# Scale and offset of the residual rows behind three layer norms, on GpSimd instead of VectorE

## What is computed

```
def layer_norm(x, g, b):
    xf = x.astype(jnp.float32)
    mu = jnp.mean(xf, -1, keepdims=True)
    var = jnp.mean(jnp.square(xf - mu), -1, keepdims=True)
    return ((xf - mu) * lax.rsqrt(var + LN_EPS) * g.astype(jnp.float32) + b.astype(jnp.float32)).astype(x.dtype)
```

## Time and profile before

| what | value |
|---|---|
| runs | 901.79, 896.52, 902.04 us; median 901.79 |
| span of the profiled execution | 904.2 us (no separate time is given for it) |
| TensorE busy | 849.0 us, 94% |
| VectorE busy | 720.1 us, 80% |
| ScalarE busy | 505.4 us, 56% |
| GpSimd busy | 76.5 us, 8% |
| mean granted TensorE clock | 0.988 of full speed |

### The profile page before, as it was taken

One profiled execution on the slowest core, in us unless ns is written; L12 is line 12 of the kernel. 1 busy time (PEld: TensorE's weight loads), 2 busy tenths in 40 slices (PEclk: granted clock), 3 DMA queues, 4 the chain that ended last, 5 costly groups with the idle time before them and its releaser, 6 DMA issues.

```text
span 904.2 us, 14872 instructions
## 1 busy us (share of the span) xinstructions
PE 849.0 (94%) x5722; PEld 773.1 (86%) x5722; DVE 720.1 (80%) x1140; ACT 505.4 (56%) x875; POOL 76.5 (8%) x121
## 2 busy tenths in 40 slices
PE   3899999999999999999999999999889999999985
PEld 3777779999999979999798989999779899889974
DVE  4777988888878878889888788676768866789897
ACT  2226657454345465468473445544475767756993
POOL 3110100010000000032000022010000000000000
PEclk9999999999999999999999999999989999999999
DMA  9988775788887748985847789987534784456621
GB/s 319 368 276 313 254 250 163 235 278 283 296 317 269 257 163 304 381 317 202 310 165 255 275 254 279 277 233 248 184 117 147 243 281 165 139 168 211 224 101 47
DMA packets 124998, 216.31 MB, mean 239 GB/s; under 512 B 12507, under 2 KB 98247, under 8 KB 118784
## 3 DMA queue, kind: packets, MB, share of 16 engines
q1 hardware_dynamic: 108156, 133.48, 44.5%
q0 software_dynamic: 13808, 73.51, 23.3%
q10 hardware_dynamic: 2964, 8.37, 2.8%
HBM read 214.18 MB, written 1.15 MB: 238 GB/s over the span
## 4 chain that ended last, share of the span: by engine, by line
PE 38%; DVE 30%; DMA 13%; ACT 12%; issue 7%; POOL 0%; DVEq 0%; ACTq 0%; POOLq 0%
DVE w_lo L1758 8%; DMA raw<-in_ffn_w_in 6%; DMA modraw<-in_mod_w 5%; DVE modsum L1790 5%; PE bank L586 5%; PE bank L588 5%; PE bank L587 5%; PE bank L592 4%; PE bank L594 4%; PE bank L593 4%; ACT w_hi L1200 4%; DVE of L1790 3%; PE bank L691 2%; ACT kk L1262 1%; DMA raw<-in_moba_w_in 1%
## 5 line engine op out<-in xcount | busy, mean ns | idle before, releaser
L1758 DVE TENSOR_TENSOR w_lo<-raw,w_hi 128x1024 fp32r<-128x1024 f32 (+1 forms) x236 | 276.0, 1205 | 66.1 <-ACT w_hi L1200 65.8
L586 PE MATMUL bank<-h_hi,w_hi 128*128 128x256 f32 x1072 | 306.5, 286 | 5.3 <-DVE w_lo L1758 3.0
L588 PE MATMUL bank<-h_hi,w_lo 128*128 128x256 f32 x1072 | 303.2, 283 | 0.0
L587 PE MATMUL bank<-h_lo,w_hi 128*128 128x256 f32 x1072 | 303.2, 283 | 0.0
L1200 ACT ACTIVATE w_hi<-raw 128x1024 fp32r<-128x1024 f32 (+1 forms) x236 | 236.6, 1036 | 63.3 <-DMA raw<-in_moba_w_in 20.0
L586 PEld LDWEIGHTS bank<-h_hi,w_hi 128*128 128x128 f32 x1072 | 205.5, 192 | 7.9 <-issue 5.1
L587 PEld LDWEIGHTS bank<-h_lo,w_hi 128*128 128x128 f32 x1072 | 205.6, 192 | 1.3 <-issue 0.5
L588 PEld LDWEIGHTS bank<-h_hi,w_lo 128*128 128x128 f32 x1072 | 205.5, 192 | 0.0
L592 PE MATMUL bank<-w_hi,o_hi 128*128 128x512 f32 x304 | 121.9, 401 | 7.2 <-ACT w_hi L1200 3.3
L594 PE MATMUL bank<-w_hi,o_lo 128*128 128x512 f32 x304 | 118.6, 390 | 0.0
L593 PE MATMUL bank<-w_lo,o_hi 128*128 128x512 f32 x304 | 118.5, 390 | 0.0
(11 more groups left out here) (323 smaller groups left out, 1259.3 us busy)
## 6 DMA issues: line engine op xcount, KB each, us to landing
raw<-in_ffn_w_in SPq DMA_DIRECT2D x88, 512.0 KB, 6.3
modraw<-in_mod_w POOLq DMA_DIRECT2D x32, 1024.0 KB, 6.9
raw<-in_ffn_w_out SPq DMA_DIRECT2D x44, 512.0 KB, 7.7
modraw<-in_ada_w POOLq DMA_DIRECT2D x16, 1024.0 KB, 5.5
raw<-in_attn_w_in SPq DMA_DIRECT2D x26, 512.0 KB, 5.5
raw<-in_moba_w_in SPq DMA_DIRECT2D x24, 512.0 KB, 8.9
modraw<-in_mod_w POOLq DMA_DIRECT2D x20, 512.0 KB, 5.1
modraw<-in_ada_w POOLq DMA_DIRECT2D x16, 512.0 KB, 4.7
```

The source lines that it names most:

```text
L586: pe.matmul(dst, cut(hi(u)), a_hi, start=first, stop=False, skip_group_check=True)
L587: pe.matmul(dst, cut(hi(u)), a_lo, start=False, stop=False, skip_group_check=True)
L588: return pe.matmul(dst, cut(lo(u)), a_hi, start=False, stop=last, skip_group_check=True)
L1758: dve.tensor_tensor(lo(v), raw_unit(v), hi(v).bitcast(F32), ALU.subtract).then_inc(sem("w_lo_ready"), 1)
```

## The change

The twelve instructions of update are removed from VectorE. GpSimd gets two functions, gained (multiply by the gain row) and shifted_rows (add the offset row), each for one tile of 128x1024, called four times per layer norm between its transfers. A gained waits for the rows g and b (rows_in) and for TensorE having turned all normalised rows (xn_turned); a shifted_rows waits for the gained of its tile. block_sum of the next norm, ScalarE's ln_rows(1) and the clearing of vv now wait for x_offset, a count of the finished shifted_rows.

```diff
--- before.py
+++ after.py
@@ -537,7 +537,23 @@
             pool.wait_ge(sem("bias_row"), 1)
             pool.dma_start(ebias, probT[0:8, 0:CAUSAL].rearrange("h (q j) -> h q j", q=1).broadcast_to(
                 [8, SKEW, CAUSAL])).then_inc(sem("ebias_out"), 16)
-            modulation(KT + 2, 4 * KT)
+            modulation(KT + 2, 3 * KT + 2)
+
+            def gained(n, t):
+                pool.wait_ge(sem("rows_in"), 32 * n + 32)
+                pool.wait_ge(sem("xn_turned"), 4 * turn_index[n] + 4)
+                pool.tensor_tensor(xrows(t), xrows(t), gain_row[n], ALU.mult).then_inc(sem("x_gained"), 1)
+
+            def shifted_rows(n, t):
+                pool.wait_ge(sem("x_gained"), 2 * n + t + 1)
+                pool.tensor_tensor(xrows(t), xrows(t), offset_row[n], ALU.add).then_inc(sem("x_offset"), 1)
+
+            gained(0, 0)
+            gained(0, 1)
+            modulation(3 * KT + 2, 3 * KT + 4)
+            shifted_rows(0, 0)
+            shifted_rows(0, 1)
+            modulation(3 * KT + 4, 4 * KT)
 
             pool.wait_ge(sem("dist_ready"), 2)
 
@@ -550,14 +566,28 @@
             pool.wait_ge(sem("w_used"), unit0("ukv", 1) + 2)
             alibi_table(0)
             alibi_table(1)
-            modulation(4 * KT, 7 * KT - 3)
+            modulation(4 * KT, 5 * KT + 5)
+            gained(1, 0)
+            modulation(5 * KT + 5, 5 * KT + 6)
+            gained(1, 1)
+            modulation(5 * KT + 6, 5 * KT + 7)
+            shifted_rows(1, 0)
+            modulation(5 * KT + 7, 6 * KT)
+            shifted_rows(1, 1)
+            modulation(6 * KT, 7 * KT - 3)
             for h in range(2, HEADS - 1):
                 alibi_table(h)
             modulation(7 * KT - 3, 7 * KT - 2)
             alibi_table(HEADS - 1)
-            modulation(7 * KT - 2, 8 * KT)
+            modulation(7 * KT - 2, 7 * KT + 2)
+            gained(2, 0)
+            gained(2, 1)
+            modulation(7 * KT + 2, 7 * KT + 4)
+            shifted_rows(2, 0)
+            shifted_rows(2, 1)
+            modulation(7 * KT + 4, 8 * KT)
             pool.wait_ge(sem("head_out"), 16)
-            pool.wait_ge(sem("x_updated"), 3)
+            pool.wait_ge(sem("x_offset"), 6)
             pool.memset(vv[:, :], 0.0).then_inc(sem("vv_zero"), 1)
             pool.wait_ge(sem("ebias_out"), 16)
             pool.wait_ge(sem("alibi"), 8)
@@ -1516,7 +1546,7 @@
                 product("moba_in", i)
                 moba_out(i)
                 if i == 0:
-                    act.wait_ge(sem("x_updated"), 1)
+                    act.wait_ge(sem("x_offset"), 2)
                     act.wait_ge(sem("h_ready"), 16)
                     ln_rows(1)
 
@@ -1843,6 +1873,8 @@
                 t, h = b // 2, b % 2
                 if b == 0:
                     dve.wait_ge(sem("fold_summed"), fold_n[0])
+                    if 1 <= p <= 3:
+                        dve.wait_ge(sem("x_offset"), 2 * p)
                 if b < 3:
                     dve.wait_ge(sem("acc_done"), 3 * p + b + 1)
                 else:
@@ -1926,20 +1958,6 @@
                 inverse(n, 1)
                 normed(n)
                 low(n)
-
-            def update(n, step):
-
-                t = step % 2
-                dve.wait_ge(sem("rows_in"), 32 * n + 32)
-                if step < 2:
-                    link(dve.tensor_tensor(xrows(t), xrows(t), gain_row[n], ALU.mult))
-                else:
-                    ins = dve.tensor_tensor(xrows(t), xrows(t), offset_row[n], ALU.add)
-                    if t:
-                        ins.then_inc(sem("x_updated"), 1)
-                        dve.wait_ge(sem("x_updated"), n + 1)
-                    else:
-                        link(ins)
 
             def rms_norm(n, p):
                 block_sum(p, 0, False)
@@ -1986,7 +2004,6 @@
                 inverse(4, 1)
                 dve.wait_ge(sem("x_full"), 4)
                 normed(4)
-                dve.nop().then_inc(sem("x_updated"), 1)
                 low(4)
 
             def attention(kind, pair, bias_of, beside=lambda t: None, after=lambda t: None):
@@ -2069,8 +2086,6 @@
                     dve.tensor_tensor(tiles(o_lo, s, s + 2), tiles(gated, s, s + 2),
                                       tiles(o_hi, s, s + 2).bitcast(F32), ALU.subtract).then_inc(
                                           sem("ff_g_ready"), 1)
-                    if i < 4:
-                        update(2 * l, i)
                     if l == 1 and i == 1:
                         fold(6, (2, 3), (2, 3))
                     if l == 0 and i == 5:
@@ -2230,8 +2245,6 @@
                 modulate(1)
 
             def moba_after(t):
-                if 0 <= t < 4:
-                    update(1, t)
                 if 4 <= t < 9:
                     modulate(1)
 
```

## The result

The median of five runs went from 901.79 us (896.52 to 905.88) to 916.80 us (915.01 to 917.68). The ratio is 1.0170, with a 95% interval from 1.0147 to 1.0193: the change costs 15 us, and the predicted range ended at 911. Profiled executions can be set against each other: spans of 904.2 and 914.8 us. (A run's time is its span plus about 1.8 us: 914.8 belongs to 916.56. By that the profiled execution of before is the run of 905.88 us, 4.1 above its median.)

The account below looks back on a forecast made before the run. The prediction took TensorE as the bound, so VectorE's time counts only where TensorE waits for it. Losses of 4.8 us less gains of 1.34 and 0.8 gave + 2.7 on 901.8, so 904.5 us, range 898.5 to 911.

Parts of the forecast that it names:

- the price per instruction: VectorE time lost to each GpSimd multiplication running beside it behind norms 0 and 2: taken as 1.2 us.
- the two scalings: VectorE's loss beside an alibi table, scaled by GpSimd's time to 0.8 us or by elements read to 1.65 us.
- the standstill rival: Behind norms 0 and 2 VectorE waits for GpSimd's whole instruction: + 12 us, 913.8 us, chance 0.14.
- 1.53 us beside a table: Profile row of a w_lo beside the first alibi table, 1.53 us instead of 1.22; taken as evidence against a full stop.
- a price of about 2.5: VectorE loss in us per GpSimd instruction from which the standstill would make the kernel slower by over 1%.
- The other additions and those of norm 1: GpSimd's additions outside FFN 1 and its norm 1 work: claimed to cost nothing, as TensorE has no wait for VectorE there.
- the late-queue rival: In the MoBA input products GpSimd delays transfers 45 to 48 by 1 to 2 us each: 907.5 us, chance 0.07.
- side effect: TensorE idle for several microseconds may be granted the lower clock, adding to the standstill; no size given.
- In MoBA 0.8: Gain from removing four updates ahead of TensorE's 1.51 us wait late in MoBA: 0.8 us, between nothing and 1.51.
- In FFN 1, 1.34: Gain in FFN 1 from removing four updates, after VectorE's loss beside GpSimd's two additions: 1.34 of 2.96 us.
- the wait of 1.66 us: TensorE's wait for VectorE at the start of step 2 of FFN 1: 1.62 us of it was to stay.
- the other two waits: TensorE's waits for VectorE at the starts of steps 3 and 4 of FFN 1, 0.36 and 0.94 us: both to go.

Follow-up runs that it names:

- experiment 5: Changed kernel with GpSimd's multiplications of norm 0 replaced by one-input ones, all norm 1 work and norm 2's multiplications by memsets: 904.32 us, ratio 1.0015.
- experiment 2: Changed kernel with norm 1's four instructions back on VectorE, norms 0 and 2 left on GpSimd: 913.68 us, ratio 1.0133.
- experiment 4: Changed kernel with twelve idle matmuls on TensorE in each of the two stalls behind norms 0 and 2: 914.46 us, ratio 1.0128.
- Experiment 3: Kernel before, with two unused VectorE reductions of about the held time behind each of norms 0 and 2, nothing on GpSimd: 910.59 us, ratio 1.0095.
- experiments 1 and 6: Changed kernel with GpSimd's work for norms 0 and 2 placed later, 907.74 us; the same with norm 1 also back on VectorE, 903.99 us.
- experiment 7: Kernel before, with norm 2's updates moved on VectorE to steps 3 and 4 of FFN 1, nothing on GpSimd: 901.16 us, ratio 0.9974.
- experiment 8: Changed kernel with each GpSimd multiplication cut into four of 128x256: 912.10 us, ratio 1.0099 to the kernel before.

## Why the prediction was wrong, point by point

**The step that failed: the price per instruction.** "I take 1.2, between the two scalings" from a least of 0.2 and a most of "VectorE stands still while GpSimd works". It was the most: 2.04 and 2.15 us behind norm 0, 2.2 for a held w_lo. The mechanism of the standstill rival was right, though it took 3.2 us as GpSimd's duration where 2.4 to 2.6 were measured. The two scalings rested on one row, 1.53 us beside a table, that was read as "not stopped". That row was of an instruction with one input, and experiment 5 shows that this kind holds for a part of its time only. The row with two inputs that was needed did not exist, and the nearest one was of another kind, not only of another size.

The price alone would not have left the range. With 2.1 us in the prediction's own sum 4 x 2.1 - 0.8 = 7.6 us give 909.4 us, and the threshold of "a price of about 2.5" for a loss over 1% was not reached either. Two terms that the sum had at nothing took it past 911: norm 1 with 4.2 us and the clock behind norms 0 and 2 with 4 us.

**What spoke for it.** The Trainium skill (SBUF — State Buffer, section "Who interferes with whom") spoke for the standstill, and was given 0.14 because of that one row. The rows of this case now agree with it for two-input instructions. The skill's figure for the duration (GPSIMD Engine Reference, section 3.1, an estimated 2.2 us) was nearer to the measured 2.37 to 2.57 than the 3.2 that was taken from the table.

**A place left out of the sum.** "The other additions and those of norm 1 lie where TensorE has no wait for VectorE": for norms 0's and 2's additions nothing was lost, for norm 1 it is false. That place costs 4.2 us (345 to 392; experiment 2 takes it away), more than a quarter of the result. TensorE showed no wait during the products, but a fold stands at their end that needs VectorE's last sum, and it had 0.76 us of wait before. Four holds made it 3.39. A stretch without waits has slack, and the slack has to be followed to the next instruction that needs the delayed engine. What was foreseen of this place held: transfers 45 to 48 are released by VectorE's sums (3.65 us idle, above), not delayed by GpSimd, and the late-queue rival did not occur.

**The clock.** It was named only as a side effect that "could add" to the standstill after "several microseconds" of idleness. Here two stalls of 1.69 and 1.82 us with 0.5 us of work between them came before it, and experiment 4 puts the price at 2 us for each of two places. Experiment 3 shows that it needs no GpSimd.

**What comes back.** In MoBA 0.8 was predicted and 0.9 came, but that is luck: the same stretch (392 to 452) changed by - 0.4 to + 0.3 us in the four kernels that kept norm 1's updates on VectorE, and by 0.0 to - 0.4 in the other four that moved them. In FFN 0 the prediction found no wait for VectorE; it overlooked the one of 0.84 us at 323.89, which went with and without the change (above), so nothing came from the change there. In FFN 1, 1.34 was predicted and 3.6 came, but by another way, and the wait of 1.66 us that was to stay went too. Experiment 3 has 2.9 with all updates still on VectorE, so most of it is the stall's own: TensorE had lost 6.1 us where VectorE lost 4.2, so VectorE was ahead when the w_lo were due. The other kernels fit that (less comes back where TensorE lost no more than VectorE: 2.2 in experiment 4), but no experiment tests it by itself. With the stall gone and only GpSimd's instructions left (experiments 1 and 6) nothing came back. The waits themselves were worth 3.6 us (experiment 7), not the 2.96 of their sum. Idle time is counted from the modelled end of the matmul before: at 493.05 it starts, its end stands at 493.33, the next starts at 494.99 and the one after it 0.19 us later. At 0.12 us a matmul these two steps would be 1.9 us shorter, not 1.66, and the other two waits have the same 0.2 us on top.

**The sum again.** The prediction's terms and what the table has for them:

| term | predicted | measured |
|---|---|---|
| VectorE held behind norms 0 and 2 | + 4.8 | + 8.0 (experiment 4) |
| lower clock behind norms 0 and 2 | 0 | + 4.2 |
| norm 1 | 0 | + 4.2 |
| FFN 1 | - 1.3 | - 3.6 |
| MoBA attention | - 0.8 | - 0.9 |
| not of the change (end + 1.5, elsewhere - 0.6) | 0 | + 0.85 |
| sum | + 2.7 | + 12.7 |

The prediction's distance between span and median is no part of the miss, since its 2.7 us were in effect added to the median.

**Range and chances.** The range left the standstill out, with 0.14; as its own 913.8 us had no clock and no norm 1 in it, but a duration too long, it came within 3 us of the measured 916.8 by errors that cancel.

**Still open.** The 1 to 2 us between the sum of the trace and the difference of the medians; why the half-clock stretch near the end (893.4 us) is in nine traces and not in the one of before; why one-input instructions let VectorE go before they end.

## What to carry to other kernels

Before moving work from VectorE to GpSimd, list what VectorE does in that time: each cast or two-input SBUF instruction that meets a two-input GpSimd instruction waits until it ends, so the move takes back more than it gives (20.3 us held for 14.6 us removed). Put such work only where TensorE has no wait **and** none at the next synchronisation behind it. Instructions that read one operand from PSUM were not held. First try moving the instruction on its own engine to a step with slack: that was the only edit here that gained.

## What the runs showed of the hardware

- GpSimd on 128x1024 in float32: 2.37 to 2.57 us with two inputs, 2.77 with one, 1.83 us for a memset of 128x2048. Where a held w_lo was still being made when the second of a pair began, the second took 3.3 to 3.4 us (pairs of 5.8 to 5.9 us), so GpSimd is slowed as well.
- A two-input GpSimd instruction held casts and two-input VectorE instructions on SBUF for all of its remaining time (2.0 to 2.2 us), and did not hold taps with one operand in PSUM. A memset held casts alone. A one-input one held both kinds for about 0.74 us at a time. Held time stands in the duration of the VectorE instruction.
- Two stalls of TensorE close together were followed by half clock: two of 1.6 to 1.8 us by 3.4 us (experiment 3, norm 0, 0.86 granted over 12 us) to 6.8 us (0.72 over 12 us), 0.85 and 0.97 us by 3.4 us (experiment 5, norm 2). One of 3.39 us was followed by 3.4 us. With idle matmuls in the stalls the clock stayed full, and in quarters (experiment 8) it stayed full behind the norms too.
